# The samples' convolution five slots later in each head of a one-core decoder layer

## The reference, cut to what matters

```
h = rmsnorm(x, norm_mix_w) * (1.0 + sc1) + sh1
z = h @ w_in + b_in
q_raw, f_raw, i_raw, og_raw, glu_a, glu_b, gate_a, gate_b = split(z)
o_a, s_new = hgrn2_branch(q_raw, f_raw, i_raw, og_raw, ...)      # S_t = diag(f_t) S_{t-1} + k_t v_t^T
u = glu_a * sigmoid(glu_b)
y = depthwise_conv(concatenate([buf, u]), dw_w) + dw_b           # 31 taps
x = x + g1 * (concatenate([sigmoid(gate_a) * o_a, sigmoid(gate_b) * silu(layernorm(y))]) @ w_out)
x = x + g2 * swiglu_ffn(rmsnorm(x) ...)
```

## Time and profile before

| what | value |
|---|---|
| median of 3 runs | 1994.35 us |
| the profiled execution's own time | 1993.56 us |
| its span | 1991.8 us |
| PE busy | 1942.2 us, 98% |
| DVE busy | 1309.9 us, 66% |
| ACT busy | 671.9 us, 34% |
| mean granted clock of PE | 0.991 |

### The profile page before, as it was taken

How to read it: one execution, slowest core, us unless ns; L and a number is a source line. 1 busy time by engine, 2 the same in 40 slices (tenths; PEclk the granted TensorE clock), 3 DMA queues, 4 the chain that set the end, 5 groups by cost and what they waited for, 6 DMA issues and landing times.

```text
span 1991.8 us, 39824 instructions
## 1 busy us (share of the span) xinstructions
PE 1942.2 (98%) x16182; PEld 1881.7 (94%) x16182; DVE 1309.9 (66%) x1800; ACT 671.9 (34%) x1090; POOL 233.6 (12%) x256
## 2 busy tenths in 40 slices
PE   7999999999999999999989999999999999999998
PEld 6999999999999999998989999999999999999998
DVE  6698879796979697967775655554455444465543
ACT  6221313131314132223853323333333333333333
POOL 2300100000010001022131683400000000000000
PEclk8999999999999999999999999999999999999999
DMA  8722222313232322223276534444445444445443
GB/s 258 230 58 81 68 73 59 90 45 95 61 90 65 83 69 73 76 76 122 96 219 205 178 106 137 138 137 133 139 129 159 141 135 137 135 138 156 137 130 112
DMA packets 417242, 237.40 MB, mean 119 GB/s; under 512 B 16375, under 2 KB 411287, under 8 KB 417072
## 3 DMA queue, kind: packets, MB, share of 16 engines
q1 hardware_dynamic: 416672, 234.48, 40.3%
q10 hardware_dynamic: 416, 0.72, 0.1%
HBM read 211.91 MB, written 24.11 MB: 118 GB/s over the span
## 4 chain that ended last, share of the span: by engine, by line
PE 84%; DVE 6%; ACT 3%; DMA 3%; POOL 2%; issue 1%; SPq 0%; DVEq 0%; ACTq 0%; POOLq 0%
PE Z L883 41%; PE Z L901 32%; PE R L920 2%; PE R L976 1%; PE Z L848 1%; DVE w_lo L1301 1%; ACT w_hi L1795 1%; PE R L926 1%; DVE ta L1466 1%; PE R L1002 1%; PE R L1009 1%; DVE k L1330 1%; DMA mbuf<-merged_scratch 1%; PE R L1011 1%; DMA xrow<-in_x_prompt_dram 1%
## 5 line engine op out<-in xcount | busy, mean ns | idle before, releaser
L1795 ACT ACTIVATE w_hi<-w_raw 128x1024 fp32r<-128x1024 f32 (+1 forms) x316 | 329.9, 1044 | 940.1 <-PE Z L883 482.2
L1301 DVE TENSOR_TENSOR w_lo<-w_raw,w_hi 128x1024 fp32r<-128x1024 f32 (+1 forms) x305 | 382.1, 1253 | 377.6 <-ACT w_hi L1795 369.3
L901 PE MATMUL Z<-h_hi,w_hi 128*128 128x352 f32 x1488 | 499.7, 336 | 2.4 <-issue 1.3
L901 PE MATMUL Z<-h_hi,w_lo 128*128 128x352 f32 x1488 | 478.4, 321 | 0.0
L901 PE MATMUL Z<-h_lo,w_hi 128*128 128x352 f32 x1488 | 477.7, 321 | 0.0
L883 PE MATMUL Z<-h_hi,w_hi 128*128 128x352 f32 x1056 | 342.3, 324 | 1.0 <-DVE w_lo L1301 1.0
L883 PE MATMUL Z<-h_hi,w_lo 128*128 128x352 f32 x1056 | 339.0, 321 | 0.0
L883 PE MATMUL Z<-h_lo,w_hi 128*128 128x352 f32 x1056 | 338.5, 321 | 0.0
L1449 DVE SCALAR_TENSOR_TENSOR yb<-up,vec,yb 128x1024 f32 (+1 forms) x240 | 310.5, 1294 | 28.7 <-DVE yb L1449 3.7
L901 PEld LDWEIGHTS Z<-h_hi,w_hi 128*128 128x128 f32 x1488 | 279.5, 188 | 19.9 <-issue 16.4
L901 PEld LDWEIGHTS Z<-h_lo,w_hi 128*128 128x128 f32 x1488 | 280.3, 188 | 0.5 <-issue 0.5
(11 more groups left out here) (304 smaller groups left out, 2455.7 us busy)
## 6 DMA issues: line engine op xcount, KB each, us to landing
w_raw<-in_w_ffn_in_dram SPq DMA_DIRECT2D x132, 512.0 KB, 3.8
w_raw<-in_w_in_dram SPq DMA_DIRECT2D x64, 512.0 KB, 4.9
w_raw<-in_w_out_dram SPq DMA_DIRECT2D x48, 512.0 KB, 3.9
w_raw<-in_w_ffn_out_dram SPq DMA_DIRECT2D x48, 512.0 KB, 3.7
aw<-in_w_ada_dram SPq DMA_DIRECT2D x32, 512.0 KB, 4.0
w_raw<-in_w_ffn_out_dram SPq DMA_DIRECT2D x24, 384.0 KB, 3.3
ada_w<-in_w_ada_dram SPq DMA_DIRECT2D x16, 512.0 KB, 6.4
mbuf<-merged_scratch SPq DMA_DIRECT2D x32, 176.0 KB, 4.0
```

Source lines behind the costliest of these rows:

```text
L901: last = mm(out, w[:, kt, :], x[:, kt, cols], start=kt == 0 and m == 0, stop=kt == NJ - 1 and m == 2)
L1301: st.tell(V.tensor_tensor(w_lo[b.par][:, 0:n, :], w_raw[b.par][:, 0:n, :], w_hi[b.par][:, 0:n, :].bitcast(F32), ALU.subtract), w_split, b. ...
L1795: A(w_hi[b.par][:, 0:n, :], w_raw[b.par][:, 0:n, :], ACT.Copy).then_inc(w_hi_ready, 1)
```

## The change

`conv_samples` moves from slot 8 to slot 13 in heads 1 to 7. In head 0 it stays in slot 17. The taps of the prompt start in slot 9 as before, which had been written as "behind the slot of the samples".

```diff
-CONV_SLOT, CONV_SLOT0 = 8, 17
+TAP_SLOT, SAMPLE_SLOT, SAMPLE_SLOT0 = 9, 13, 17
...
-                conv_at = CONV_SLOT0 if first else CONV_SLOT
+                conv_at = SAMPLE_SLOT0 if first else SAMPLE_SLOT
...
                         if slot == conv_at:
                             conv_samples(h)
-                        if slot > CONV_SLOT:
-                            if h.i is None and slot == CONV_SLOT + 1:
+                        if slot >= TAP_SLOT:
+                            if h.i is None and slot == TAP_SLOT:
                                 dve.wait_ge(xt_first if first else xt_stored, 16)
                             for tap in itertools.islice(taps, 1 if first and slot in SLOW_SLOTS else 2):
                                 conv_tap(tap, h)
```

## The result

The changed kernel takes 1999.48 us (median of 22 runs, 1996.28 to 2002.68), the kernel before 1994.73 (22 runs beside them, 1993.31 to 1998.54). The ratio is 1.0022, with a 95% interval of 1.0015 to 1.0028: 3.0 to 5.6 us slower, where 6.3 were forecast. The profiled execution has a span of 1999.1 us against 1991.8.

A forecast was written before the change was run, and what follows sets the result against it. PE, busy 98%, was taken as the bound, held by DVE, which has no pause from slot 8 to slot 25. Loop heads +6.57 and head 1 -0.27 gave +6.3 us: 2000.0 us predicted, range 1996 to 2004.

The forecast's parts named there:

- The wait at fill 10: PE's stall for `level_up(5)`, 0.75 us in head 2, goes; PE then runs 0.75 ahead.
- The pause: DVE stands idle 1.44 us before slot 9's work, where the convolution had been, until fill 9 is done.
- The order of the waits: DVE's delay holds PE at fills 18, 22 and 24: 0.28, 0.58, then 1.18 us behind the old times.
- the samples' price in slot 13: The convolution's cost on DVE between two taps in slot 13: 3.98 us, with a settled gap included.
- the lower bound of 3.73: The convolution's cost from below: its 3.73 us in slot 8, without the idle before it.
- The second heads of an iteration: Their stall at fill 10 was 0.17 us larger, so each costs 1.01 us instead of 1.18.
- Head 1: DVE's 2.36 us of idle before `w_lo` and `f` hold the delay; only the stall's removal is left, -0.27 us.
- The sum: Six loop heads cost 6.57 us, less 0.27 in head 1: +6.3 us on the profiled execution's 1993.56.
- (a): Rival: DVE's delay doesn't reach fills 18 and 24, only stalls go; 5.3 us faster, 1988.3; chance 0.08.
- (b): Rival: the delay reaches fill 18 but is worked off before fill 24; 1993.5 to 1996.5 us; chance 0.14.
- (c): Rival: DVE also waits in slots 10 and 11, a loop head costs 2.1 us; about +12, 2006; chance 0.08.

The follow-up runs named there:

- slot9: The changed kernel with the samples' convolution in slot 9, before the first tap, in heads 1 to 7 instead of slot 13: 2001.05 us.
- slot17: The changed kernel with the samples' convolution in slot 17, behind the emptying of fill 16, in heads 1 to 7: 2002.31 us.
- pad9: The kernel before with one more, unread DVE operation in slot 9 of heads 1 to 7, nothing moved: ratio 1.0016 to the kernel before.
- hole3: The changed kernel with two taps put into slot 8 in heads 1 to 7, one taken from each of slots 12 and 13: 1990.15 us.
- hole: The changed kernel with taps from slot 8 on in heads 1 to 7, still two in every later slot: 2017.32 us.
- nosamples: The samples' convolution left out in all heads, one small operation in slot 13 instead, outputs not those of the reference: 1989.37 us.
- win: The changed kernel with taps from slot 8, samples in slot 17, one tap in slots 17 to 21 and 23, the rest in 24 to 26: 1990.02 us.
- win2: The same kernel as win, run once more: 1989.49 us.
- hole2: The changed kernel with two taps put into slot 8 in heads 1 to 7, one taken from each of slots 9 and 10: ratio 1.0010 to the kernel before.
- oldtail: The kernel before with one tap in each of slots 20 to 23 and the rest in slots 24 to 26: ratio 1.0004 to the kernel before.

## Why the prediction was right

- **The wait at fill 10.** It went in all loop heads and in head 1, as worked out: `level_up(5)` starts 1.39 us after DVE is free, and PE gained 0.82 for the 0.75 that were counted.
- **The pause.** 1.39 us measured for 1.44. That it is what costs is shown from two sides: slot9, slot17 and pad9 have other places and other work and the same loss, and hole3, with the pause filled and no new one, has none.
- **The order of the waits.** Fills 18, 22 and 24 became the places, as forecast: PE was 0.08, 0.34 and 0.85 behind, for 0.28, 0.58 and 1.18. Each is smaller by 0.20 to 0.33.
- **The mis-sized term** is the samples' price in slot 13, 3.98. From the taps' end at 293.25 to the next tap at 297.17 are 3.92 us, less a gap of 0.15: 3.77. The gap in front of L1471 isn't there, and neither is a register instruction in front of it, as the changed kernel's order shows; I take the second for the reason of the first. The trace thus came out near the lower bound of 3.73, which is also the cost by the Trainium skill's sentence (VectorE: DVE Perf Modes, The DRAIN you can't avoid). The settled gaps of taps are still 0.15 in this trace, so the Trainium skill's reason is not borne out. A further 0.08 was absorbed in front of `f`, where `f` now starts before `w_lo` has ended. With these two the forecast for head 2 is 1.18 - 0.21 - 0.08 = 0.89, and 0.85 was measured at its fill 24.
- **The second heads of an iteration** were to cost 0.17 less, and at fill 24 they do: counted from fill 3, it is 0.70, 0.61 and 0.75 later than before in heads 3, 5 and 7, and 0.85, 0.83 and 0.87 in heads 2, 4 and 6. What was wrong is the step behind it, that both engines are then late by the same and the head's length follows. Measured to the next head's fill 3, heads 2, 4 and 6 cost 0.82, 0.89 and 0.85, but head 7 0.81 and heads 3 and 5, which end at the loop's back edge, 0.96 and 1.15. So 4.6 of the 5.5 us stand at fill 24, and 0.9 come behind it, 0.8 of them in heads 3 and 5. In head 5 PE stood 1.1 us at the loop's branch, for nothing that the profile shows, where the longest such wait before was 0.7; in the other kernels' traces (hole apart) the longest is between 0.7 and 1.2, with the samples' work or without it, so this part can't be laid to the change. The gap of 0.44 in front of L1466 did not come back in slot 13.
- **Head 1**: -0.31 for -0.27; its 2.36 us of idle time absorbed the delay.
- **The sum**: 6.3 forecast, 4.8 measured (3.0 to 5.6), 5.5 - 0.3 = 5.2 in the heads of the trace. That 2000.0 lies 0.5 from the measured 1999.5 is in part luck: the sum gave 1999.9 for the profiled execution, and with the 0.8 by which that lies below the median it should have been 2000.7.
- **The rivals.** (a), the gain at fill 10 stays, was false for this change, but its price of 5.3 us was right: nosamples, win and win2 came out 5.9, 5.4 and 5.5 us below the kernel before. What it needs is DVE time in front of fill 24. (b), the delay worked off before fill 24, didn't happen: PE waits there for DVE's `O` in all six loop heads; (c), more pauses in slots 10 and 11, didn't happen here; hole2 had one, of 1.07 us in front of slot 11.

Open is the rest of the profiled span's +7.3 us: 0.8 before head 1 and 1.4 behind the heads. It is no larger than the spread of the runs (6.4 us for the changed kernel), and no experiment was made for it.

## What to carry to other kernels

An engine that is 66% busy can be without a pause for the stretch that decides. Before an operation is moved on it, look at what it does in front of the old place: if it would have waited there anyway, the operation was free there, and moving it adds its whole length to a stretch that has no idle time. A wait that you then see on the bound engine (here at fill 10) may be cheaper than the ones that replace it. It was won here in two ways: by other work put into the pause and taken from where the engine is behind, so that no new pause arises (hole3, over 4 us off the loop heads), or by work that moves behind the last release as well (win, 4.6). Moving work behind the last release alone won nothing (oldtail).

## What the runs showed of the hardware

In hole PE stood for nearly two microseconds at the loop's back edge behind head 3 and then ran at a lower clock. Its timeline of PE:

```profile
452.90 0.32 PE L901 MATMUL Z<-h_hi,w_lo 128*128 128x352 f32 x1
455.10 0.47 PE L901 MATMUL Z<-h_hi,w_hi 128*128 128x352 f32 x1 [1.88 <-issue]
455.37 0.50 PE L901 MATMUL Z<-h_lo,w_hi 128*128 128x352 f32 x1
455.66 0.50 PE L901 MATMUL Z<-h_hi,w_lo 128*128 128x352 f32 x1
...
460.69 0.49 PE L920 MATMUL R<-ident,v 128*128 128x128 f32 x3 [0.91 <-issue]
```

And its table of stretches, with the columns as above:

```profile
447.00:455.00 8.00, 6.22 (x41) 5.93 (x38) 4.55 (x7) 1.74 (x2) 0.00 (x0) 1.00 0.61 165
455.00:461.00 6.00, 4.99 (x21) 4.82 (x22) 1.23 (x1) 0.34 (x1) 5.42 (x2) 0.72 0.56 162
```

The matmuls start 0.29 us apart for 3.5 us and not 0.16, and the granted clock of the stretch is 0.72, so for about half of it PE had the lower of its two levels, 1.2 GHz. From fill 24 at 446.85 to the next head's first fill there are 13.8 us, 3.8 more than before: the two waits are 2.8 where 0.66 stood before, and twelve distances of 0.29 in place of 0.16 are 1.6.

In the stretch with the first wait, 447 to 455, the DMA engines moved 165 GB/s. In the kernel before PE stood at this branch before 448.25, and from 445 to 450 they moved 7 GB/s. In hole the last tap comes a slot earlier, and with it the load that SP issues behind `conv_done`. That DMA traffic delays PE's instructions at the branch would fit, but nothing was run to show it.

The length of a wait alone doesn't tell whether the clock falls. Hole has nine waits of PE of 1.77 to 2.10 us in the loop heads. Behind five of them the clock went to the lower level: the 1.88 above, those of 2.06, 1.92 and 2.01 at fill 18 in heads 2 to 4, and one of 2.10 at L920 behind head 5's branch. It fell at once or up to 1.5 us after PE had gone on. Behind the other four, 1.77 at head 5's branch and 1.92, 2.02 and 1.92 at fill 18 in heads 5 to 7, it stayed at 1.00. Behind the waits of 0.75 and 0.92 at fill 10 in heads 2 and 3 of the kernel before the granted clock was 1.00.
